# The recurrent layer's gate products: eight full-precision fp32 matmuls in a block replaced by twenty-four fp32r ones on split operands

## The reference, cut to what matters

```python
def block_diag_linear(x, w, b):
    xb = x.reshape(x.shape[:-1] + (RNN_BLOCKS, RNN_BLOCK_W))      # 16 blocks of 128
    y = jnp.einsum('bsni,nio->bsno', xb, w)
    return y.reshape(x.shape) + b

def rg_lru(x, ga_w, ga_b, gx_w, gx_b, lam):
    r = jax.nn.sigmoid(block_diag_linear(x, ga_w, ga_b).astype(jnp.float32))
    i = jax.nn.sigmoid(block_diag_linear(x, gx_w, gx_b).astype(jnp.float32))
    log_a = -LRU_C * r * jax.nn.softplus(-lam.astype(jnp.float32))
    ...

def rglru_layer(h, w_in, conv_w, conv_b, ga_w, ga_b, gx_w, gx_b, lam, w_out):
    proj = h @ w_in
    gate_br, rec_br = jnp.split(proj, [D_RNN], axis=-1)
    xr = causal_depthwise_conv(rec_br, conv_w, conv_b)
    y = rg_lru(xr, ga_w, ga_b, gx_w, gx_b, lam)
    return (jax.nn.gelu(gate_br) * y) @ w_out
```

## Time and profile before

| | |
|---|---|
| median of 3 runs | 2320.46 us (2320.1 to 2320.71) |
| the profiled execution, whole | 2319.96 us |
| its span, first to last instruction | 2318.2 us |
| PE busy | 2299.3 us (99%) |
| DVE busy | 1579.7 us (68%) |
| ACT busy | 1240.5 us (54%) |
| POOL busy | 206.8 us (9%) |

### The profile page before, as it was taken

How to read it: one execution, slowest core, us unless ns; L and a number is a source line. 1 busy time by engine, 2 the same in 40 slices (tenths; PEclk the granted TensorE clock), 3 DMA queues, 4 the chain that set the end, 5 groups by cost and what they waited for, 6 DMA issues and landing times.

```text
span 2318.2 us, 38109 instructions
## 1 busy us (share of the span) xinstructions
PE 2299.3 (99%) x13164; PEld 2002.4 (86%) x13164; DVE 1579.7 (68%) x1958; ACT 1240.5 (54%) x1701; POOL 206.8 (9%) x188
## 2 busy tenths in 40 slices
PE   8999999999999999999999999999999999999999
PEld 6888888988888888888888888898888888888888
DVE  7766776577777777755556778667777777774443
ACT  5655555465555555544444776556555555553332
POOL 5620001230000000000000100222000000000000
PEclk9999999999999999999999999999999999999999
DMA  7656435545555555565555555645555555556554
GB/s 271 201 195 200 132 120 180 173 155 173 193 188 181 189 185 199 187 198 189 189 190 183 181 190 177 197 136 181 177 196 193 186 181 187 197 186 199 188 188 159
DMA packets 118943, 426.95 MB, mean 184 GB/s; under 512 B 13600, under 2 KB 14496, under 8 KB 118864
## 3 DMA queue, kind: packets, MB, share of 16 engines
q1 hardware_dynamic: 117072, 418.36, 54.4%
q0 software_dynamic: 1792, 7.52, 1.0%
HBM read 423.73 MB, written 2.10 MB: 184 GB/s over the span
## 4 chain that ended last, share of the span: by engine, by line
PE 91%; DVE 5%; ACT 2%; issue 1%; DMA 0%; SPq 0%; ACTq 0%; DVEq 0%
PE ps L345 49%; PE ps L349 24%; PE ps L385 7%; PE ps L390 4%; DVE w_lo L318 2%; PE ps L330 2%; PE ps L366 2%; ACT w_hi L312 1%; PE ps L650 1%; PE ps L837 1%; DVE y_buf L1623 1%; DVE y_buf L1628 0%; PE ps L635 0%; DVE xg_hl L1270 0%; DVE u_buf L1616 0%
## 5 line engine op out<-in xcount | busy, mean ns | idle before, releaser
L318 DVE TENSOR_TENSOR w_lo<-raw,w_hi 128x1024 fp32r<-128x1024 f32 x788 | 961.4, 1240 | 500.3 <-ACT w_hi L312 496.0
L312 ACT ACTIVATE w_hi<-raw 128x1024 fp32r<-128x1024 f32 x787 | 810.8, 1054 | 559.8 <-PE ps L349 418.6
L345 PE MATMUL ps<-xg_hl,w_hi 128*128 128x512 f32 x3328 | 1046.8, 396 | 3.4 <-DVE w_lo L318 3.4
L349 PEld LDWEIGHTS ps<-xg_hl,w_lo 128*128 128x128 f32 x3328 | 625.2, 188 | 147.8
L349 PE MATMUL ps<-xg_hl,w_lo 128*128 128x256 f32 x3328 | 653.8, 278 | 0.0
L345 PE MATMUL ps<-a_hl,w_hi 128*128 128x512 f32 x1920 | 603.0, 395 | 0.6 <-DVE a_hl L1441 0.6
L345 PEld LDWEIGHTS ps<-xg_hl,w_hi 128*128 128x128 f32 x3328 | 506.9, 189 | 4.4 <-DVE w_lo L318 4.2
L349 PEld LDWEIGHTS ps<-a_hl,w_lo 128*128 128x128 f32 x1920 | 360.7, 188 | 85.3
L349 PE MATMUL ps<-a_hl,w_lo 128*128 128x256 f32 x1920 | 377.1, 278 | 0.0
L345 PEld LDWEIGHTS ps<-a_hl,w_hi 128*128 128x128 f32 x1920 | 292.2, 189 | 0.7 <-DVE w_lo L318 0.7
L1157 ACT ACTIVATE y_buf<-u_buf,fconv 128x256 f32<-128x256 f32 x176 | 96.4, 595 | 231.3 <-DVE u_buf L1616 231.3
(11 more groups left out here) (197 smaller groups left out, 1528.9 us busy)
## 6 DMA issues: line engine op xcount, KB each, us to landing
raw<-in_w_stream SPq DMA_DIRECT2D x787, 512.0 KB, 4.1
bias<-in_rel_bias POOLq DMA_DIRECT2D x4, 768.0 KB, 6.1
memT<-in_mem_t POOLq DMA_DIRECT2D x4, 512.0 KB, 5.9
gate_w<-in_gate_w POOLq DMA_DIRECT2D x4, 512.0 KB, 3.9
out_t<-xT SPq DMA_DIRECT2D x8, 256.0 KB, 4.4
xT<-in_x_t SPq DMA_DIRECT2D x2, 512.0 KB, 9.2
xT<-in_x_t SPq DMA_DIRECT2D x3, 256.0 KB, 7.4
raw<-in_w_stream SPq DMA_DIRECT2D x2, 256.0 KB, 3.1
```

The costliest lines, as they stand in the source:

```text
L312: nc.scalar.activation(w_hi[:, s, :], raw[:, s, :], ACT.Copy).then_inc(hi_done, 1)
L318: nc.vector.tensor_tensor(w_lo[:, s, :], raw[:, s, :], w_hi[:, s, :].bitcast(F), ALU.subtract).then_inc(lo_done, 1)
L345: nc.tensor.matmul(ps[:, bank + m, :], w_hi[:, s, w], both, start=start and k == ks[0], stop=False, skip_group_check=True)
L349: last = nc.tensor.matmul(ps[:, bank + m, SEQ:2 * SEQ], w_lo[:, s, w], x[:, xk, 0, :], start=False, stop=stop and k == ks[-1], skip_group_ ...
```

## The change

Both operands of the gate products are split into fp32r high and low parts, as the streamed weights are. For each block ACT makes `gate_hi` in step u = 1 and `xr_hi` in step u = 3; DVE makes `gate_lo` in step u = 2 (over `gate_w`, in place) and `xr_lo` in step u = 3. All four are single instructions over 128 x 1024 numbers. PE multiplies high by high, high by low and low by high, each accumulated in the same place, and waits for `gate_lo_ready` and `xr_lo_ready` where it waited for `gate_w_in` and `xr_ready`.

```diff
+        gate_hi = at("gate_hi", R2 + 16384, [2, 4, P], R)
+        gate_lo = at("gate_lo", R2 + 12288, [2, 4, P], R)
+        xr_hi = at("xr_hi", FFN + size([4, SEQ + 2]), [4, SEQ], R)
+        xr_lo = at("xr_lo", R2 + 20480, [4, SEQ], R)
...
-                    pe.wait_ge(gate_w_in, times(16, i, 16))
-                    pe.wait_ge(xr_ready, times(4, i, 4))
+                    pe.wait_ge(gate_lo_ready, times(1, i, 1))
+                    pe.wait_ge(xr_lo_ready, times(1, i, 1))
                     for m in range(4):
                         for w in range(2):
-                            last = nc.tensor.matmul(ps[:, 4 + m, w * SEQ:(w + 1) * SEQ], gate_w[:, w, m, :], xr[:, m, :],
-                                                    start=True, stop=True)
+                            for q, (a, b) in enumerate(((gate_hi, xr_hi), (gate_hi, xr_lo), (gate_lo, xr_hi))):
+                                last = nc.tensor.matmul(ps[:, 4 + m, w * SEQ:(w + 1) * SEQ], a[:, w, m, :], b[:, m, :],
+                                                        start=q == 0, stop=q == 2)
                     last.then_inc(gates_ps, 1)
...
+                if u == 1:
+                    act.wait_ge(gate_w_in, times(16, i, 16))
+                    A(gate_hi[:, :, :, :], gate_w[:, :, :, :], ACT.Copy).then_inc(gate_hi_ready, 1)
+                if u == 3:
+                    act.wait_ge(xr_ready, times(4, i, 4))
+                    A(xr_hi[:, :, :], xr[:, :, :], ACT.Copy).then_inc(xr_hi_ready, 1)
...
+                if u == 2:
+                    dve.wait_ge(gate_hi_ready, times(1, i, 1))
+                    V.tensor_tensor(gate_lo[:, :, :, :], gate_w[:, :, :, :], gate_hi[:, :, :, :].bitcast(F),
+                                    ALU.subtract).then_inc(gate_lo_ready, 1)
+                if u == 3:
+                    dve.wait_ge(xr_hi_ready, times(1, i, 1))
+                    V.tensor_tensor(xr_lo[:, :, :], xr[:, :, :], xr_hi[:, :, :].bitcast(F), ALU.subtract).then_inc(xr_lo_ready, 1)
```

More of the change, by code:

```diff
@@ L241, in trunk @@
         cross_ready, u_scaled, c_scaled, g_scaled = sem("cross_ready"), sem("u_scaled"), sem("c_scaled"), sem("g_scaled")
+        gate_hi_ready, gate_lo_ready = sem("gate_hi_ready"), sem("gate_lo_ready")
+        xr_hi_ready, xr_lo_ready = sem("xr_hi_ready"), sem("xr_lo_ready")
         gates_ps, r_ready, i_ready, t_ready = sem("gates_ps"), sem("r_ready"), sem("i_ready"), sem("t_ready")
```

## The result

The changed kernel takes 2333.39 us (median of 6 executions, 2331.88 to 2337.51), the kernel before 2320.53 us beside it. The ratio is 1.0057, 95% interval 1.0047 to 1.0067: slower by 0.57%, where 0.38% was forecast, and 0.39 us above the upper end of the range. The executions scatter over 5.6 us, those of the kernel before over 0.6 us. The profiled one took 2333.44 us, with a span of 2331.7 us and a mean granted clock of 0.998.

What follows compares the result with a forecast made beforehand. PE, busy for 99% of the span, was taken as the bound. 11.11 us lost less 2.30 gained, +8.81 on the profiled 2319.96, gave 2328.8 us; the median lying 0.5 us higher, the forecast was 2329.2 us, range 2326 to 2333.

Steps and rivals of the forecast that it cites:

- The gain on PE: At the gates, 24 fp32r products take 2.88 us instead of 3.455, saving 0.575 us a block, 2.30 us in all.
- The loss before the gates: PE waits at the gates for DVE's `xr_lo`, 2.64 to 2.90 us late in each block, 11.11 us together.
- The handing over: From the end of DVE's `xr_lo` to PE's gates: 0.05 + 0.10 us, 0.15 us a block.
- The sum: Whole kernel: 11.11 us lost at the gates less 2.30 us gained there, +8.81 us.
- What comes behind: After the gates, later splits, loads and sigmoids cause no new PE wait: nothing more lost, nothing given back.
- PE's clock falls in the new gap: Rival, 8%: each gap at the gates slows twelve matmuls, 2.5 us each, 10 us for four, time 2339 us.
- The sign: Whole kernel: slower by more than 0.2% (4.6 us) 92%, within it 7%, faster by more 1%.
- the first rival: The 8% rival that PE's clock falls after the gaps at the gates, 2339 us; a granted clock below 1.00 would show it.

Runs made afterwards that it cites:

- xr_lo_first_5: The changed kernel with `xr_lo` before the `w_lo` of step 2 and the gates one step later on PE and ACT: 2317.86 us, ratio 0.9991.
- filled: The changed kernel with eleven unused fp32r matmuls of 512 columns on PE right before its wait at the gates: 2329.1 us, ratio 1.0038.
- longer: The changed kernel with `xr_lo` behind one more `w_lo` on DVE, moved from step 3 to the start of step 4: 2340.49 us, ratio 1.0089.

## Why the prediction was wrong

- **The gain on PE** was forecast from the earlier trace rows at 2.88 us a block for the new products. They take 2.83 us without a wait, so the gain was forecast 0.2 us too small in all (2.30 against 2.50). The Trainium skill ("FP8 and Floating Point Precision", TensorE Precision Notes) gives true fp32 four passes; by that rule, as an estimate, three quarters of 3.455, they would take 2.6 us, and the rows were the better guide.
- **The loss before the gates** was forecast at 11.11 us. DVE's order, the 1.135 us from instruction to instruction, ACT's `xr_hi` out of the way and `gate_hi` at no cost all came as worked out. The gaps are 10.4 us in all and the gates take 0.23 us longer behind a gap (3.06 against 2.83, 3.69 against 3.46), 0.9 us in all: 11.3 us. Most of the 0.23 us is no cost of the restart. Without a gap the first product starts about 0.16 us before the recorded end of the matmul ahead of it, and the chain counts from that end (1273.93, where the timeline has 1273.76); with a gap there is no such overlap, and the gap too is counted from that end. The restart itself costs 0.07 us: the second product starts 0.19 us behind the first and not 0.12. The first two products behind a gap at full clock (block 2 of the changed kernel), then without a gap (`xr_lo_first_5`):

```profile
1326.25 0.35 PE L844 MATMUL ps<-xr_hi,gate_hi 128*128 128x256 f32 x1 [2.72 <-DVE xr_lo L1754]
1326.44 0.28 PE L844 MATMUL ps<-xr_lo,gate_hi 128*128 128x256 f32 x1
```

```profile
1273.76 0.28 PE L844 MATMUL ps<-xr_hi,gate_hi 128*128 128x256 f32 x1
1273.88 0.28 PE L844 MATMUL ps<-xr_lo,gate_hi 128*128 128x256 f32 x1
```

  From `xr_lo` to PE's start are 0.14 us. The handing over is thus 0.21 us and not the 0.15 of the earlier trace rows.
- **The sum** of +8.81 us is what the profile shows without the slow clock, 8.8 us, and what `filled` measured, 2329.1 us against the forecast of 2329.2. That it is right to 0.1 us is in part luck: the loss and the gain were each forecast 0.2 us too small.
- **What comes behind**: no other new wait of PE in the section. Right.
- **The step that failed is the rival "PE's clock falls in the new gap"**, to which I gave 8%. The argument against it was that "our gap is less than half of the only one known to do so". That is no evidence: the trace had gaps up to 0.9 us and one of 6.3 us and nothing between, so that everything between was open. In the changed kernel 9 of 12 profiled gaps brought a fall, and each of its 15 executions lies at least 2.3 us above the 2329.2 of the sum. Its price was wrong the other way: I took 2.5 us for a fall from the kernel's start; it is 1.3 to 1.5 us (4.37 to 4.60 against 3.06), and 2.4 us or more where the slow stretch lasts twice as long (5.46). The warning of the Trainium skill ("TensorE: Matmul & The Clock Gate", Why this matters for your kernels), that pauses between bursts of matmuls send the clock back, was named and then set aside. The runs agree that pauses do this; the page has somewhat longer ones in mind, and that 2.42 to 2.82 us can be enough is what the runs show. By four falls of 1.4 us the rival's time would have been 2335 us, and a range up to there was called for.
- **The sign** was right (slower, 0.57% where 0.38% was forecast), and so was most of what the changed profile would show: the new row of waits, the order on DVE and the place of `xr_hi`. The gates take 3.06 us in the chain and not 2.88, and the granted clock did not stay at 1.00; the prediction named that as the sign of the first rival, and it was.

## What to carry to other kernels

Where the matrix engine is the bound and works without a break, a new wait has two prices: its length, and a stretch at half clock behind it. Here the second came at the gates behind none of 5 gaps of 1.4 to 1.7 us, behind 17 of 37 of 2.4 to 2.8 us and behind 5 of 6 above 3.1 us, and once behind 1.78 us near the kernel's start; a gap length that lies between those the trace has seen is to be priced as possible, not as excluded. A split or cast whose result the bound engine waits for belongs at the head of its step, ahead of work prepared for four units later; and moving the consumer one unit down its list may hide the wait for nothing, as it did here (2319.1 us instead of 2332.0 to 2334.4, all but 0.9 us of the wait), where making other inputs earlier did not, as that work landed on the start of the same chain.

## What the runs showed of the hardware

- A plain fp32 product of 256 columns is recorded as two matmuls and takes 0.432 us of PE, an fp32r product 0.118 us (2.83 / 24). Three fp32r products in the place of one fp32 product save 18% of PE's time for it.
- The granted clock can fall while PE rests or up to 1.4 us after it has resumed (`longer`: 1330.5 against 1329.15), and of the gaps of one execution the longest need not be the one that brings it: in the first profile those of 2.52, 2.67 and 2.47 us did and that of 2.72 us did not.
- After a wait at full clock PE's second product starts 0.19 us behind its first instead of 0.12; the rest of the 0.23 us by which the chain shows the gates longer is the overlap of recorded matmuls, which a gap takes away.
- Useless matmuls in a gap (44, 10 us of PE's time) cost nothing: the time is 2.9 to 5.3 us below that of the changed kernel, and the scatter 1.0 us instead of up to 5.6.
